# Starting products before their fourth bank is free, a key slab split in quarters, and scores that wait for their own rotation

## What is computed

```python
def swiglu(hn, w1, w3, w2):
    return (jax.nn.silu(hn @ w1) * (hn @ w3)) @ w2

kv_a = rmsnorm_2(h, norm_kv_g) @ w_kv_a          # 1024 -> 512 + 64
c_kv = rmsnorm_2(kv_a[..., :512], kv_a_norm_g)
k_rope = apply_rope(kv_a[..., 512:])             # one rotary key for all heads
kv = c_kv @ w_kv_b                               # 512 -> 8 heads x (128 key + 128 value)
cq = rmsnorm_2(hn @ w_q_a, q_a_norm_g)           # 1024 -> 768
q = cq @ w_q_b                                   # 768 -> 8 heads x (128 + 64 rotary)
sc = einsum(q, k) ; p = softmax(sc * 192 ** -0.5 + mask) ; o = p @ v
h = h + o @ w_o
h = h + swiglu(rmsnorm_2(h, norm_ffn_g), ffn_w1, ffn_w3, ffn_w2)
```

## Time and profile before

| what | value |
|---|---|
| median of 3 runs | 1558.58 us (1558.41 to 1560.11) |
| the profiled execution's own time | 1556.98 us |
| its span (first to last instruction) | 1555.1 us |
| PE busy | 1388.3 us, 89% |
| DVE, ACT, POOL busy | 720.4, 527.0, 210.8 us |
| mean granted TensorE clock | 0.945 |

### The profile page before, as it was taken

The page is one execution under the profiler, slowest core; times in us unless marked ns, Lnnn a source line. Parts: engine busy times, 40 slices in busy tenths (PEclk is TensorE's granted clock), DMA queues, the critical chain, the costliest instruction groups (busy, mean ns, idle before and its releaser), DMA issues.

```text
span 1555.1 us, 27615 instructions
## 1 busy us (share of the span) xinstructions
PE 1388.3 (89%) x11858; PEld 1167.3 (75%) x11858; DVE 720.4 (46%) x1208; ACT 527.0 (34%) x813; POOL 210.8 (14%) x173
## 2 busy tenths in 40 slices
PE   7999899897677677677999989999999999999997
PEld 7998568664344344344887979999999876899997
DVE  5365665421111121122764665555556564565644
ACT  6346453110000010012334444444345433544442
POOL 5132002100000000001000023211224200101123
PEclk9999899699888889887999999999999999999999
DMA  9332118989999999999435241454355321445340
GB/s 360 138 149 70 68 55 354 378 373 427 430 428 429 428 429 428 429 428 379 187 147 192 109 176 55 163 196 166 112 214 188 139 109 55 163 166 212 121 180 28
DMA packets 32422, 360.01 MB, mean 231 GB/s; under 512 B 5328, under 2 KB 8400, under 8 KB 10192
## 3 DMA queue, kind: packets, MB, share of 16 engines
q1 hardware_dynamic: 32336, 358.76, 57.6%
HBM read 357.70 MB, written 1.05 MB: 231 GB/s over the span
## 4 chain that ended last, share of the span: by engine, by line
PE 70%; DMA 18%; DVE 4%; ACT 3%; issue 2%; SPq 1%; POOL 1%; DVEq 0%; ACTq 0%
PE PS L541 42%; DMA expert_w<-in_w 18%; PE PS L554 5%; PE PS L995 4%; PE PS L589 3%; PE PS L1016 3%; PE PS L960 1%; DVE wl L1936 1%; SPq L395 1%; PE PS L1175 1%; PE PS L837 1%; PE PS L572 1%; PE PS L1369 1%; ACT wh L1428 1%; PE PS L694 1%
## 5 line engine op out<-in xcount | busy, mean ns | idle before, releaser
L1936 DVE TENSOR_TENSOR wl<-raw,wh 128x4096 fp32r<-128x4096 f32 (+2 forms) x67 | 272.0, 4059 | 207.4 <-ACT wh L1428 207.4
L1428 ACT ACTIVATE wh<-raw 128x4096 fp32r<-128x4096 f32 (+2 forms) x67 | 223.1, 3330 | 117.3 <-PE PS L541 111.8
L541 PE MATMUL PS<-UH,wh 128*128 128x272 f32 (+1 forms) x840 | 244.5, 291 | 14.0 <-DVE wl L1992 10.6
L541 PE MATMUL PS<-UH,wl 128*128 128x272 f32 (+1 forms) x840 | 241.5, 288 | 0.0
L541 PE MATMUL PS<-UL,wh 128*128 128x272 f32 (+1 forms) x840 | 241.0, 287 | 0.0
L995 PE MATMUL PS<-expert_w,XW 128*32 128x256 f32 x2048 | 159.1, 467 | 89.3 <-DMA expert_w<-in_w 89.0
L995 PEld LDWEIGHTS PS<-expert_w,XW 128*32 128x32 f32 x2048 | 71.1, 129 | 165.2 <-DMA expert_w<-in_w 109.3
L541 PEld LDWEIGHTS PS<-UH,wh 128*128 128x128 f32 x840 | 159.1, 189 | 15.3 <-DVE wl L1992 10.6
L541 PEld LDWEIGHTS PS<-UL,wh 128*128 128x128 f32 x840 | 159.5, 190 | 0.4
L541 PEld LDWEIGHTS PS<-UH,wl 128*128 128x128 f32 x840 | 159.2, 190 | 0.0
L2300 DVE TENSOR_TENSOR SG<-PS,SG 128x128 f32<-128x128 f32 x32 | 9.3, 292 | 274.0 <-ACT SG L1695 274.0
(11 more groups left out here) (522 smaller groups left out, 3011.1 us busy)
## 6 DMA issues: line engine op xcount, KB each, us to landing
expert_w<-in_w SPq DMA_DIRECT2D x96, 2048.0 KB, 20.4
raw<-in_up SPq DMA_DIRECT2D x22, 2048.0 KB, 8.4
raw<-in_down SPq DMA_DIRECT2D x16, 1408.0 KB, 6.0
raw<-in_ret_v SPq DMA_DIRECT2D x4, 2048.0 KB, 8.7
raw<-in_ret_gate SPq DMA_DIRECT2D x4, 2048.0 KB, 8.4
raw<-in_ret_o SPq DMA_DIRECT2D x4, 2048.0 KB, 9.4
raw<-in_ret_qk SPq DMA_DIRECT2D x3, 2048.0 KB, 8.6
raw<-in_w_in_ga SPq DMA_DIRECT2D x2, 2048.0 KB, 8.4
```

The lines of the kernel that those rows point to most:

```text
L541: mm = pe.matmul(gbank(g)[:, c0:T], w[:, c:c + P], x(k)[:, c0:], start=(k == 0 and j == 0), stop=(k == nk - 1 and j == 2))
L1428: act.activation(WH[n % 2][:, 0:w], raw(n)[:, 0:w], ACT.Copy).then_inc(hi_done, 1)
L1936: dve.tensor_tensor(wl_of(n)[:, 0:w], raw(n)[:, 0:w], WH[n % 2][:, 0:w].bitcast(F32), ALU.subtract).then_inc(lo_done, 1)
```

## The change

- In `products_as_split` with four units, blocks 0 to 3 are made for units 0 to 2 first, then blocks 0 to 3 for unit 3 alone, then blocks 4 to 7 for all four. Each unit's bank is awaited at its own first matmul.
- `kn` is made by `product`, unit by unit, with one wait for the last key latent ahead of it.
- ACT and DVE split slab `kv_a` in quarters. The first quarter goes ahead of the latent of `krq` 3, the other three behind it.
- The rotations' banks are 1, 0, 1, 2, 3. The scores of head h wait for the rotation of their own pair of heads; the scores of step 1 and the transposes of steps 0 and 1 wait until DVE has read the rotation in their bank.
- On DVE the second rotation moves behind `qn0`'s scaling, and the fourth query rotation and the first quarter of `kv_b` move behind the first maxima.

```diff
+                order = [(k, u) for k in range(nk) for u in range(count)]
+                if count == 4:
+                    order.sort(key=lambda ku: (ku[0] >= 4, ku[0] < 4 and ku[1] == 3))
+                for k, u in order:
+                    if k == 0:
+                        bank_free(g + u)
+                    if u == 0:
+                        before(k)
+                        if parts is not None:
+                            pe.wait_ge(nhi_done, parts[0] + k + 1)
+                            pe.wait_ge(nlo_done, parts[1] + k + 1)
...
             slab_ready(n)
-            products_as_split(UNIT0["kn"], 4, n, 4, *CK, None, 0,
-                              lambda k: pe.wait_ge(freed["dve"], FREED[UNIT0["kvc"] + k][1]))
+            pe.wait_ge(freed["dve"], FREED[UNIT0["kvc"] + 3][1])
+            for u in range(4):
+                product(UNIT0["kn"] + u, n, 4 * u, 4, *CK)
...
-                if j >= 4:
-                    pe.wait_ge(rot_free, 10 + j - 3)
-                pe.matmul(sbank(j % 4)[:, c0:T], rot[:], t, start=True, stop=True).then_inc(rot_mm, 1)
+                if j == 2:
+                    pe.wait_ge(rot_free, 11)
+                pe.matmul(sbank(j - 1 if j else 1)[:, c0:T], rot[:], t, start=True, stop=True).then_inc(rot_mm, 1)
...
-            pe.wait_ge(rot_done, 15)
...
                 if t == 0:
+                    pe.wait_ge(rot_done, 10 + 2 + h // 2)
                     pe.wait_ge(freed["dve"], max(FREED[UNIT0[f"qn{h}"]][1], FREED[ready[f"kn{h}"]][1]))
+                elif h == 0:
+                    pe.wait_ge(rot_free, 13)
...
-                if i >= 2:
+                if i < 2:
+                    pe.wait_ge(rot_free, 14 + i)
+                else:
                     pe.wait_ge(at_ca, base + i - 1)
...
@@ ACT
-            for u in range(3):
+            for u in range(2):
                 latent(UNIT0["krq"] + 1 + u, u, CQH, "qa", late)
-            hi(FIRST_SLAB["kv_a"])
+            hi_part(FIRST_SLAB["kv_a"], 0)
+            latent(UNIT0["krq"] + 3, 2, CQH, "qa", late)
+            for q in range(1, 4):
+                hi_part(FIRST_SLAB["kv_a"], q)
...
@@ DVE
-            for u in range(3):
+            for u in range(2):
                 latent(UNIT0["krq"] + 1 + u, u, CQH, CQL, "qa", late, 44 + u + 1)
-            lo(FIRST_SLAB["kv_a"])
+            lo_part(FIRST_SLAB["kv_a"], 0)
+            latent(UNIT0["krq"] + 3, 2, CQH, CQL, "qa", late, 44 + 3)
+            for q in range(1, 4):
+                lo_part(FIRST_SLAB["kv_a"], q)
...
-            for j in range(2):
-                rotated(11 + j, QR[:, j, META:], ROT_M, META)
+            rotated(11, QR[:, 0, META:], ROT_M, META)
             scaled_out(UNIT0["qn0"], QN[:, 0, late], RQS, late)
-            for j in range(2, 4):
+            for j in range(1, 3):
                 rotated(11 + j, QR[:, j, META:], ROT_M, META)
             scaled_out(UNIT0["qn1"], QN[:, 1, late], RQS, late)
-            lo_part(FIRST_SLAB["kv_b"], 0)
...
             mla_maxima(0)
+            rotated(14, QR[:, 3, META:], ROT_M, META)
+            lo_part(FIRST_SLAB["kv_b"], 0)
```

More of the change, by code:

```diff
@@ L576, in products_as_split @@
             def products_as_split(g, count, n, nk, xh, xl, parts, c0=0, before=lambda k: None):
-                for u in range(count):
-                    bank_free(g + u)
                 wh, wl = WH[n % 2], wl_of(n)
[L581 to L592, removed]
+                order = [(k, u) for k in range(nk) for u in range(count)]
[9 more added lines that the diff above has]
+                            pe.wait_ge(nlo_done, parts[1] + k + 1)
+                    c = (u * nk + k) * P
+                    for j, (w, x) in enumerate(((wh, xh), (wh, xl), (wl, xh))):
+                        mm = pe.matmul(gbank(g + u)[:, c0:T], w[:, c:c + P], x(k)[:, c0:],
+                                       start=(k == 0 and j == 0), stop=(k == nk - 1 and j == 2))
+                    if k == nk - 1:
+                        mm.then_inc(unit_done, 1)
             def total(count, acc, bank, c0=0):
@@ L2008, in _ @@
             link(dve.tensor_tensor(sinw[:], sinw[:], rs[:], ALU.mult))
+            ROT_BANKS = (1, 0, 1, 2, 3)
             def rotated(j, t, scratch, c0=0):
@@ L2014, in rotated @@
                 dve.wait_ge(rot_mm, j + 1)
-                dve.tensor_tensor(scratch[j % 2][:, c0:], sbank((j if j < 10 else j - 10) % 4)[:, c0:T], sinw[:, c0:],
+                dve.tensor_tensor(scratch[j % 2][:, c0:], sbank(j % 4 if j < 10 else ROT_BANKS[j - 10])[:, c0:T], sinw[:, c0:],
                                   ALU.mult).then_inc(rot_free, 1)
```

## The result

The median is 1545.62 us (1544.76 to 1545.86, 4 runs) against 1558.68 (1558.41 to 1560.11, 4 runs) before: 13.1 us less, ratio 0.9913 with a 95% interval of 0.9896 to 0.9931. Two later comparisons on other occasions gave 0.9931 (0.9913 to 0.9948) and 0.9927 (0.9903 to 0.9952). Applied to the medians of before, these ratios are 13.6 us for the first comparison and 10.7 and 11.4 us for the later two; the bare differences of the medians are 13.1, 12.3 and 11.2 us. Forecast was 1550.0, in the range 1548.3 to 1552.7: the way was right, the size too small. The profiled executions stand at 1556.98 and 1545.86, 11.1 us apart.

What follows compares the result with a forecast made beforehand. PE was taken as the bound, with 70% of the span, so its pauses count in full. Gains 1.00 + 0.30 + 1.40 + 4.14 + 1.75 = 8.59 us, from 1558.58, gave 1550.0, range 1548.3 to 1552.7.

Steps and rivals of the forecast that it cites:

- up0: Before `up0`: PE's wait for bank 3, held by `rwo`'s last unit, goes; gain 1.00 us.
- kvc: Before `kvc`: it starts 0.78 us early, most is given back at `krq`; gain 0.30 us.
- kn: Before `kn`: pause of 2.55 us goes and the clock behind it is full (1.53); gain taken 4.14 us.
- first scores: Before the first scores: PE no longer waits for all five rotations; gain 1.75 us.
- The list of five pauses: Pauses of PE before `up0`, `kvc`, `up1`, `kn` and the first scores: 1.00, 1.00, 1.50, 2.55 and 1.75 us.
- The quarters: Slab `kv_a` in quarters has 2.2 us to spare; with POOL's additions ready by 1221.0 at worst, before 1221.72.
- up1: Before `up1`: PE starts at 1353.51, its second group is just in time; gain 1.40 of the 1.50 us.
- the margin of 0.05: At `up1`'s second group: bank 0 is read at 1365.55, PE gets there at 1365.6, just in time.
- The first transposes: At `mla_turned(0)`: DVE's scaling ends at 1260.9, PE wants it at 1261.18; in time by 0.3 us.
- the median lies 1.6 above the profiled execution: Step from sum to time: the whole gain is taken from the runs' median, 1558.58 - 8.59 = 1550.0 us.
- after pauses of 1.0 to 1.8 us the clock did not fall: Argument against the rival of a partial gain (clock stays low or fourth quarter late: 1551.5 or 1552.4 us), chance 18%.

Runs made afterwards that it cites:

- better: The changed kernel with slabs of `krq` and each `up`'s second group in quarters, output weights' last quarter a step earlier; 1544.89 us beside 1546.90.
- before_b: The kernel before, unchanged, run once more for a second profile; ratio to before 1.0006 (0.9992 to 1.0020).
- before_c: The kernel before, unchanged, run a third time; ratio to before 1.0010 (0.9995 to 1.0025).
- extra_waits: The kernel before with one more fulfilled wait of PE before each head's scores; ratio 1.0006 (0.9995 to 1.0018).
- fill_pauses: The kernel before with 18 extra matmuls ahead of `kn` and 12 ahead of the first scores, in pauses that stay; ratio 0.9977 (0.9967 to 0.9988).
- rotations_only: The rotation part alone: the kernel before with only the rotations' banks, their DVE order and the scores' waits changed; ratio 0.9992 (0.9982 to 1.0002).
- The slab part alone: The kernel before with only `kn`'s products unit by unit and slab `kv_a` in quarters; ratio 0.9985 (0.9975 to 0.9994).

## Why the prediction was right in its steps and wrong in its time

**up0, kvc, kn, first scores: right**, to 0.06 us each (table). The list of five pauses lacked a sixth, the one before `wo`, worth 0.49 us on the spot. The forecast that most of `kvc`'s gain is given back at `krq` held: 0.36 is kept, since DVE's pass of `krq`'s slab runs 1192.09 to 1196.51 and the latent only follows.

**The quarters: right.** DVE in the changed kernel, the first quarter and then the other three, and POOL's additions beside them:

```profile
1210.52 1.23 DVE L1961 TENSOR_TENSOR wl<-raw,wh 128x1024 fp32r<-128x1024 f32 x1 [2.96 <-ACT wh L1451]
...
1212.11 4.14 DVE L1961 TENSOR_TENSOR wl<-raw,wh 128x1024 fp32r<-128x1024 f32 x3
...
1210.83 1.52 POOL L2695 TENSOR_TENSOR ACCQ<-ACCQ,NSQ 128x256 f32<-128x256 f32 x1 [2.59 <-ACT NSQ L1486]
1214.32 0.86 POOL L2695 TENSOR_TENSOR ACCQ<-ACCQ,NSQ 128x256 f32<-128x256 f32 x1 [1.97 <-ACT NSQ L1486]
```

The slab is ready at 1216.25, 1.5 us before PE comes for it (2.2 forecast, 0.7 at worst). POOL no longer waits out a whole pass: 1.52 and 0.86 us where one addition had been held behind 4.42. The last quarter in turn was held up behind POOL's addition of 1214.32 to 1215.17: begun at 1214.49, it took 1.76 us, where the one before it took 1.22. By the Trainium skill, page "SBUF — State Buffer", section "SBUF: two separate sides", whichever of the two starts first keeps the shared port pair for its whole instruction; the trace agrees, now in both directions.

**up1: nearly**, 1.28 instead of 1.40. The start came 1.50 early, but the second group then waited 0.45 for bank 0 instead of 0.1 (row at 1355.72, released by DVE's `FT`). DVE was as forecast: its reciprocal ended 11.76 behind `mo`'s last matmul, against 11.74 before. PE was ready for the second group 11.8 behind its start and not 12.06, since the total was counted with its duration of 0.6 and not with its distance: the margin of 0.05 was worked out too finely. `better` takes this wait away.

**The first transposes: right.** DVE's scaling ends at 1252.66 (my 1260.9 less the shift of 8.1 says 1252.8), PE comes at 1252.91.

**What failed: the step from the sum to the time.** It is the sentence that the median lies 1.6 above the profiled execution and that "I take the gain from it", with, among the rivals, "after pauses of 1.0 to 1.8 us the clock did not fall". Both took one execution for all. So the sum has a term at nothing, the falls of the clock behind the pause before the first scores. The 1.6 us were not an offset to carry along; they look like time that the median execution spends and the profiled one did not: the profiled executions of `before_b` and `before_c`, 1559.10 and 1558.65, lie within 0.5 us of their runs' medians, and both have the fall. Over 14 profiles, seven have the pause of 1.87 (2.08 in the one of `extra_waits`) before the first scores. Six of them show a fall behind it, of 1.5 us (two) or 3.0 us (four), and the one without is the one I had read. Of the seven without the pause, or with it filled, none shows a fall there. The mean over the seven with it is 15 / 7 = 2.1 us. So my estimate of the mean gain is 8.4 + 2.1 = 10.5 us, or 11.0 with `wo`'s 0.5 if that lasts; the two later comparisons gave 10.7 and 11.4, though their intervals, from 8.1 and from 7.5 us up, leave room for 8.4 too. What shows the falls are the profiles, and `fill_pauses`. Taken from 1558.6, 11.0 gives 1547.6, already below the range; the measured 1545.62 lies another 2 us lower. The Trainium skill, page "TensorE: Matmul & The Clock Gate", section "Part 1: The HAM clock gate", says of the other transition, from the low level up to the full one, that its point varies from run to run. In these traces the falls differ too: behind the same pause none, 3.0 and 3.0 us in three profiles of one kernel.

**What stays open.** The part up to `rwo`'s last product took 981.8 to 988.4 us over the 14 profiles, in code that is the same but for the waits at `zb` and `wo`: 985.3 to 986.8 in the four of the kernel before and of `extra_waits`, 983.2 to 985.1 in the three of the changed kernel, 981.8 to 988.4 in the others. The means are 985.8 for the seven with the old `products_as_split` and 984.2 for the seven with the new one. I take the first pair's 2.7 us as `wo`'s 0.5 and such scatter, and the 13.1 us of the first comparison as 11.0 and some of it; that is argued, not shown. The rotation part alone should have gained 1.8 and the fall, some 3.9, and was measured at 1.2 (-0.3 to 2.8); its profile shows another fall near the first output products, and `fill_pauses` shows one 13 us later. The slab part alone falls short as well: it gains 4.2 us at `kn` and leaves the pause before the first scores as it was, but 2.3 (0.9 to 3.9) were measured. So the two parts alone give less than their pauses and falls add up to, while the whole gives what they add up to. That a fall taken away in one place makes a later one likelier would fit this, but it was not tried.

## What to carry to other kernels

Count a pause of TensorE twice: its length, and the chance that the clock falls behind it; one profile shows only one draw of that, so where the profiled execution is faster than the median of the runs, look for what it was spared, and take a second profile before the sum is trusted. When units share an order of work, leave the one whose bank comes free last for later: it costs no instruction and hides the read-out behind 36 matmuls. Look for every caller of the helper that is changed, those with another number of units too: `kn` and `wo` were both overlooked here.

## What the runs showed of the hardware that I had not expected

A pause of 1.87 us was followed by low clock in six of seven executions (granted clock 0.53 to 0.76 over the next 7 us), while pauses of 1.13 before `up0` and `kvc`, and of 1.6 before `up1`, were not in any of the seven profiles that have them. The pause of 2.67 before `kn` was in all five. Length alone does not order them: the short pause before the first output products (0.92 from start to start) had low clock behind it in one profile, that of `rotations_only`. What follows differs too: behind the pause of 1.87 come the scores' and transposes' short matmuls, behind `kvc` and `up1` products without a break. Which of the two decides was not tried. 30 matmuls whose result nobody reads made the kernel 3.6 us faster (1.9 to 5.1).
